# Hybrid decoder step: FFN 1's gate and up products as seven block products for eight, ahead of all of down

## The chip, the cores and the metric

The kernel runs on one core of a Trainium2 chip, as one program. The metric is the device time of an execution in microseconds (us), the median of three runs. The engines are TensorE (PE in the rows; PEld is its weight load), VectorE (DVE), ScalarE (ACT), GpSimd (POOL) and SyncE (SP); SP and ACT issue the DMA transfers.

## The reference, cut to what matters

1032 tokens (1024 of a prompt, 8 samples) of width 1024 go through FFN 1, a mixing stage (RWKV and S5 branches, merged by gates) and FFN 2, all in f32. The change concerns FFN 1 and the norm ahead of it:

```python
def rmsnorm(x, g):
    y = xf * lax.rsqrt(jnp.mean(xf * xf, axis=-1, keepdims=True) + NORM_EPS)
    return (y * g.astype(jnp.float32)).astype(x.dtype)

def swiglu(x, w_gate, w_up, w_down):
    return (jax.nn.silu(x @ w_gate) * (x @ w_up)) @ w_down

x = x + 0.5 * swiglu(rmsnorm(x, p['g_ffn1']), p['ffn1_gate'], p['ffn1_up'], p['ffn1_down'])
```

`FFN_DIM` is 2816, that is 22 tiles of 128 columns of gate and 22 of up.

## The kernel before

Activations lie transposed: x is 8 tiles (`DT`) of 128 features by 1032 tokens. A matmul in f32 is made as three matmuls of rounded parts: every operand is split into a high part (fp32r) and the low rest, and hi x hi, hi x lo and lo x hi are added up in PSUM. So weights and activations each need a copy (high) and a subtraction (low) before TensorE can use them.

**FFN 1** (`ffn_block`, from line 363) works in four groups of 6, 6, 5 and 5 tiles (`FFN_GROUPS`). In a group each turn makes one gate tile and one up tile: two products (`product`, line 199) of 8 k-tiles x 3 parts x 3 token blocks of 344 columns, 72 matmuls each. GpSimd splits the weights of each (lines 179 and 182, `split_units`). VectorE scales both sums by the norm's factor `rstd` (lines 455, 458), multiplies (463) and makes the low part (466); ScalarE makes the silu (534) and the high part (536). After the turns of a group come eight down products over its tiles, which VectorE adds to x in SBUF (492; 482 in the last group). At the program's start ScalarE and VectorE make the high and low parts of g*x, and the squares and their sums in transposed form (lines 254, 270, 273); TensorE adds the sums over the partitions and spreads `rstd`.

**S5 setup.** VectorE also computes tables for the later S5 branch, some 520 small steps of 16 to 256 columns, each waiting for the one before (`s5_setup_dve`, `Steps.do`; lines 600 to 760). They are dealt out by an estimate of their time: up to `SLOT_NS` = 9000 ns of them at the end of a turn (`spend`). Whenever a table is ready ScalarE stores it to DRAM at the beginning of a later turn (`store`, line 837), where it waits for `su_ready`.

**FFN 2** (`strassen_ffn`) has another form already. Gate and up of a tile are one pair; the activations are two token halves (516 columns) by even and odd feature tiles, and a pair takes seven block products of 4 k-tiles x 3 parts x 2 blocks of 258 columns, 24 matmuls each (line 3487, `PROD`), on sums and differences of the blocks. The operands b11, t1, t2, b21, t3, b22 and t4 are made once. For each pair ScalarE makes seven high parts of weights (3366), GpSimd seven low parts (3170) and four sums of weight blocks (3173), 128x512 each. High and low parts lie in a ring of four places, so the parts of a product can be made only a few products ahead. The pair's results: ScalarE copies three partial sums out of PSUM (3394, 3404, 3409) and makes two silus of half width (3417); VectorE adds (`g1a`, `u2a`, `g2a`), scales and multiplies, nine steps of 516 columns (3304 to 3327). TensorE's seventh product (n = 6) waits for `u2a`, the first of the next pair for `g1a`. ScalarE's order in an even pair is: ... copy, high part, silu 1 (waits for VectorE's `g1m`), high part, silu 2; weight work stands behind the silu in its queue. Finished tiles go to DRAM and come back for down (`a_spilled`).

Of the kernel before, what the change touches and what calls it, by code (L numbers as in the profile page):

```python
# [97 lines left out]
def plan(nc, g):  # L98
# [58 lines left out]
    g.a_tiles = 0  # L157

# [91 lines left out]
def square_act(act, g, n, k, tmp):  # L250

    if k >= 2:
        act.wait_ge(g.ssum_step, DT * n + k - 1)
    act.activation(tmp[:, k % 2, :], g.x[:, k, :], ACT.Square).then_inc(g.sq_ready, 1)


def squares_act(act, g, n, ready=None):

    for k in range(DT):
        if ready:  # L260
            ready(k)
        square_act(act, g, n, k, g.tmp)
# [3571 lines left out]
```

## Time and profile before

| | us |
|---|---|
| median of 3 runs (2458.02 to 2460.93) | 2459.64 |
| span of the profiled execution | 2458.0 |
| TensorE busy in it | 2413.0 (98%) |
| VectorE, ScalarE, GpSimd busy | 1287.0, 579.2, 1053.7 |

The profile is of one execution. Its time lies in stages: FFN 1 up to 765 us, the mixing stage up to 1736, FFN 2 to the end. Engines run beside each other, so a stage is read by the engine that is never idle there, and then by what each idle stretch of it waits for. Matmul durations in the rows overlap; the distance from start to start is the cost.

### The profile page before, as it was taken

What the parts mean: (1) busy time and instruction counts of PE and PEld (TensorE: products, weight loads), DVE (VectorE), ACT (ScalarE), POOL (GpSimd) and SP (SyncE); (2) the same over time, 40 slices, a digit from 0 to 9 for tenths busy, and PEclk for the clock granted to TensorE, in tenths of its full rate; (3) what the DMA queues carried; (4) which work ended last, traced back from release to release, by engine and by line L of the source; (5) the groups of instructions that cost most, each with busy time, mean ns of one, the idle gap of its engine ahead of it and who ended that gap; (6) DMA issues with size and microseconds to landing.
All of it is one profiled execution on the core that took longest, in us unless ns stands there. A gap on an engine that the chain in (4) does not pass through costs nothing. (4 is left out here: it accounts for less than half of the span.)

```text
span 2458.0 us, 50034 instructions
## 1 busy us (share of the span) xinstructions
PE 2413.0 (98%) x21418; PEld 2361.5 (96%) x21418; DVE 1287.0 (52%) x1843; ACT 579.2 (24%) x1084; POOL 1053.7 (43%) x604
## 2 busy tenths in 40 slices
PE   8999999999999999999998999999999999999998
PEld 8999999999999999999997888899999999999998
DVE  6851871671336255642466776666754444453225
ACT  4000010010011000010336676412433333341001
POOL 3434444344444344422340000244686868775550
PEclk9999999999999999999999999999999999999998
DMA  3111211111114432623451100062121212143211
GB/s 141 43 53 50 77 60 52 68 53 59 51 38 176 104 93 86 186 79 100 152 190 58 33 18 19 30 243 106 65 104 63 91 70 84 69 181 106 76 52 69
DMA packets 93733, 211.94 MB, mean 86 GB/s; under 512 B 16464, under 2 KB 42704, under 8 KB 92816
## 3 DMA queue, kind: packets, MB, share of 16 engines
q1 hardware_dynamic: 67184, 157.96, 19.2%
q10 hardware_dynamic: 26400, 51.82, 6.5%
q8 instruction: 115, 1.88, 0.3%
q14 instruction: 34, 0.28, 0.0%
HBM read 154.39 MB, written 54.20 MB: 85 GB/s over the span
## 5 line engine op out<-in xcount | busy, mean ns | idle before, releaser
L179 POOL TENSOR_TENSOR whi<-wraw,small 128x1024 fp32r<-128x1024 f32 (+3 forms) x134 | 227.9, 1701 | 844.9 <-PE ps L213 772.1
L213 PE MATMUL ps<-hhi,whi 128*128 128x344 f32 x1848 | 396.3, 323 | 0.0
L213 PE MATMUL ps<-hlo,whi 128*128 128x344 f32 x1848 | 392.9, 321 | 0.0
L213 PE MATMUL ps<-hhi,wlo 128*128 128x344 f32 x1848 | 391.5, 320 | 0.0
L182 POOL TENSOR_TENSOR wlo<-wraw,whi 128x1024 fp32r<-128x1024 f32 (+3 forms) x134 | 324.9, 2425 | 10.5
L213 PEld LDWEIGHTS ps<-hlo,whi 128*128 128x128 f32 x1848 | 313.4, 189 | 0.0
L213 PEld LDWEIGHTS ps<-hhi,whi 128*128 128x128 f32 x1848 | 311.1, 189 | 1.9 <-issue 0.7
L213 PEld LDWEIGHTS ps<-hhi,wlo 128*128 128x128 f32 x1848 | 309.5, 189 | 0.0
L3487 PE MATMUL ps<-t_hi,whi 128*128 128x258 f32 x704 | 143.7, 285 | 3.0 <-ACT ffn_gate L3394 1.0
L534 ACT ACTIVATE tmp<-tmp 128x1032 f32<-128x1032 f32 x22 | 23.5, 1068 | 504.2 <-DVE tmp L455 487.8
L3487 PE MATMUL ps<-t_lo,whi 128*128 128x258 f32 x704 | 142.2, 283 | 0.0
L3487 PE MATMUL ps<-t_hi,wlo 128*128 128x258 f32 x704 | 141.3, 282 | 0.0
L3170 POOL TENSOR_TENSOR wlo<-weights_sum,whi 128x512 fp32r<-128x512 f32 x66 | 92.1, 1395 | 52.7 <-ACT whi L3366 51.4
L3487 PEld LDWEIGHTS ps<-t_hi,whi 128*128 128x128 f32 x704 | 108.7, 189 | 5.0 <-POOL wlo L3170 1.7
L1784 POOL TENSOR_TENSOR sm_v<-sm_v,rw_e 128x2048 f32<-128x2048 f32 x1 | 3.6, 3622 | 253.5 <-DVEq L1547 253.5
L213 PE MATMUL ps<-ahi,whi 128*128 128x344 f32 x528 | 111.9, 320 | 0.0
L213 PE MATMUL ps<-alo,whi 128*128 128x344 f32 x528 | 111.7, 320 | 0.0
L213 PE MATMUL ps<-ahi,wlo 128*128 128x344 f32 x528 | 111.5, 319 | 0.0
L3487 PEld LDWEIGHTS ps<-t_hi,wlo 128*128 128x128 f32 x704 | 109.0, 189 | 0.0
L3487 PEld LDWEIGHTS ps<-t_lo,whi 128*128 128x128 f32 x704 | 108.9, 189 | 0.0
L492 DVE SCALAR_TENSOR_TENSOR x<-ps,x 128x1032 f32 x24 | 29.6, 1233 | 151.4 <-PE ps L213 151.4
L3487 PE MATMUL ps<-b_lo,whi 128*128 128x258 f32 x528 | 106.3, 283 | 0.0
(513 smaller groups left out, 5056.8 us busy)
## 6 DMA issues: line engine op xcount, KB each, us to landing
wraw<-ffn_up SPq DMA_DIRECT2D x44, 512.0 KB, 3.2
wraw<-ffn_down SPq DMA_DIRECT2D x40, 384.0 KB, 3.0
wraw<-ffn_up SPq DMA_DIRECT2D x11, 1024.0 KB, 4.8
weights_raw_b<-ffn_up SPq DMA_DIRECT2D x11, 1024.0 KB, 4.7
a_spilled<-ffn_gate SPq DMA_DIRECT2D x18, 516.0 KB, 2.7
a_raw<-a_spilled SPq DMA_DIRECT2D x18, 516.0 KB, 4.4
wraw<-w_mix SPq DMA_DIRECT2D x18, 512.0 KB, 3.4
gates<-gate_out ACTq DMA_DIRECT2D x16, 516.0 KB, 2.8
```

The costliest lines, as they stand in the source:

```text
L179: pool.tensor_tensor(g.whi[:, s, 0:n], g.wraw[:, s, 0:n], g.zero.to_broadcast([P, n]), ALU.add).then_inc(g.w_hi, 1)
L182: pool.tensor_tensor(g.wlo[:, s, 0:n], g.wraw[:, s, 0:n], g.whi[:, s, 0:n].bitcast(F32), ALU.subtract).then_inc(g.w_split, 1)
L213: last = pe.matmul(g.ps[:, 3 * bank_set + b, 0:BLK], w[:, s, k * P:(k + 1) * P], x(k, b), start=(k == 0 and first), stop=(k == kt - 1 and ...
L492: v.scalar_tensor_tensor(xt, acc(g, j), 0.5, xt, ALU.mult, ALU.add)\
L534: act.activation(g.tmp[:, 0, :], g.tmp[:, 0, :], ACT.Silu).then_inc(g.silu_done, 1)
L1784: st.do(pool.tensor_tensor(V, V, over(E7[:, :, sample]), ALU.mult))
L3170: pool.tensor_tensor(ring(g.wlo, n), source(n), ring(g.whi, n).bitcast(F32), ALU.subtract).then_inc(g.st_lo, 1)
L3487: last = pe.matmul(g.ps[:, b0 + c, 0:QB], ring(w, r, k), x[:, k, c * QB:(c + 1) * QB], start=start and k == 0 and first, stop=k == DT // 2 ...
```

## The change

FFN 1 gets a function of its own, `first_ffn`, in the form that FFN 2 has. All 22 pairs run ahead of all of down. Pair 0 takes eight plain block products (`FIRST_PROD`) while the operands are made, pairs 1 to 21 seven each. Every finished activation tile goes to DRAM; down reads them back in blocks of 6, 6, 6 and 4 tiles, and reads x again from its input. The norm's sums come from a second copy of x, row-major: ScalarE squares nine row tiles with a running sum (`rows_squares`), VectorE takes the root, nine TensorE products spread it. The S5 setup is dealt out anew: up to `PAIR_NS` = 5000 ns after each of pairs 2 to 20 and `DOWN_NS` = 4000 ns after a down unit. x is stored for later in eight parts during the last down units. FFN 2's semaphores get base values; its steps are the same.

The diff, cut to its core:

```diff
+FIRST_HI = [(n, q) for n in ("b11", "b21", "t1", "b22", "t2", "t3", "t4") for q in range(4)]
+FIRST_LO = FIRST_HI[:-4]
+HI0, LO0 = len(FIRST_HI), len(FIRST_LO)
+FIRST_PARTS = ((3, 0, 0), (0, 1, 0), (1, 0, 1), (2, 1, 1))
+FIRST_PROD = ((0, "b11", 2, True, None), (1, "b11", 0, True, None), (2, "b21", 4, True, None), (3, "b21", 6, True, None),
+              (0, "t1", 2, False, "p1"), (1, "t1", 0, False, "q1"), (2, "b22", 2, False, None), (3, "b22", 0, False, None))
+FIRST_BLOCKS = ((0, 6, (0, 1, 2, 3, 4, 5)), (6, 6, (6, 7, 10, 11, 16, 17)), (12, 6, (0, 1, 2, 3, 4, 5)),
+                (18, 4, (8, 9, 15, 16)))
...
+        def rows_squares(n):
+            if n < 8:
+                act.wait_ge(g.gt_in[n // 4], 16)
+                x, total = g.rows[n // 4][:, n % 4, :], g.small[:, 0, n:n + 1]
+            else:
+                act.wait_ge(g.c_in, 16 * 3)
+                x, total = g.rows_end[0:NB, :], g.small[0:NB, 0, n:n + 1]
+            act.activation(x, x, ACT.Square, accum_out=total).then_inc(g.xt_sq, 1)
...
+        def one(i, b, j, between=None):
+            pair, n = 2 * b + j, 7 * j
+            a11, a12, a21, a22 = (part(j, r, c) for r in range(2) for c in range(2))
+            lo(i, b, n)
+            pool.wait_ge(g.st_in[j], i * 16 + 16 * (b + 1))
+            total("s1", sums(0), a21, a22, ALU.add)
+            g.fst_sum.wait(pool, i, pair, "s1")
+            total("s2", sums(1), sums(0), a11, ALU.subtract)
+            lo(i, b, n + 1)
+            total("s3", a21, a11, a21, ALU.subtract)
+            lo(i, b, n + 2)
+            lo(i, b, n + 3)
+            total("s4", sums(1), a12, sums(1), ALU.subtract)
+            lo(i, b, n + 4)
+            lo(i, b, n + 5)
+            if between:
+                between()
+            lo(i, b, n + 6)
+
+        for n, (s, r, c) in enumerate(FIRST_PARTS):
...
+        for n, (s, r, c) in enumerate(FIRST_PARTS):
+            pool.wait_ge(g.st_hi, n + 1)
+            pool.tensor_tensor(place(g.wlo, s), part(0, r, c), place(g.whi, s).bitcast(F32), ALU.subtract)\
+                .then_inc(g.st_lo, 1 if n < 3 else 4)
+        for q in range(4):
+            pool.wait_ge(g.b_mixed, q + 1)
+            pool.tensor_scalar(g.x[:, 2 * q, late], g.x[:, 2 * q, late], gain(2 * q), None, ALU.mult).then_inc(g.b_scaled, 1)
...
+        setup["vector_start"](v, st)
...
+        for pair in range(2, NP):
+            j = pair % 2
+            G, U = halved(g.gate, j), halved(g.upv, j)
+            last = pair == NP - 1
+            done(v, 0, pair, 3)
+            g.fst_copy.wait(v, 0, pair, "p1")
+            on(v.tensor_tensor(G[0], two("y", j), G[0], ALU.add))
+            g.fst_up.wait(v, 0, pair, "g1a")
+            on(v.tensor_tensor(G[0], G[0], R[0], ALU.mult))
+            if last:
+                tile_low(0)
+            done(v, 0, pair, 4)
+            g.fst_copy.wait(v, 0, pair, "p5")
+            on(v.tensor_tensor(U[1], two("x", j), U[1], ALU.add))
+            g.fst_up.wait(v, 0, pair, "u2a")
+            on(v.tensor_tensor(U[1], U[1], R[1], ALU.mult))
+            if last:
+                tile_low(1)
+            done(v, 0, pair, 5)
+            g.fst_copy.wait(v, 0, pair, "u2")
+            on(v.tensor_tensor(G[1], two("z", j), G[1], ALU.add))
+            g.fst_up.wait(v, 0, pair, "g2a")
+            on(v.tensor_tensor(G[1], G[1], R[1], ALU.mult))
+            if last:
+                tile_low(2)
+            done(v, 0, pair, 6)
+            on(v.tensor_tensor(U[0], two("x", j), R[0], ALU.mult))
+            if last:
+                tile_low(3)
+            g.fst_up.wait(v, 0, pair, "u1")
+            g.fst_copy.wait(v, 0, pair, "silu1")
+            on(v.tensor_tensor(G[0], G[0], U[0], ALU.mult))
+            g.fst_copy.wait(v, 0, pair, "silu2")
+            on(v.tensor_tensor(G[1], G[1], U[1], ALU.mult))
+            if last:
+                tile_low(4)
+                tile_low(5)
+            else:
+                setup["vector"](pair, PAIR_NS)
...
+        for pair in range(2, NP):
+            j = pair % 2
+            G, U = ([halves(t[:, j, x]) for x in xa] for t in (g.gate, g.upv))
+
+            def hi(step):
+                for n in SPLIT_AT.get(7 * j + step, ()):
+                    if n < BODY or pair < NP - 2:
+                        hi_of(n, pair - j)
+
+            def silu(half):
+                g.fst_up.wait(act, 0, pair, ("g1m", "g2m")[half])
+                x = halves(g.gate[:, j, xa[half]])
+                on(act.activation(x, x, ACT.Silu))
+
+            setup["scalar"](act, pair)
+            hi(0)
+            if pair == 2:
+                full_silu(0, 1)
+            done(act, 0, pair, 0)
+            act.wait_ge(g.a_out[j], spilled[j] + 16 * (pair // 2))
+            on(act.activation(G[0], two("x", j), ACT.Copy))
+            hi(1)
+            if pair == 2:
+                full_silu(1, 2)
+            done(act, 0, pair, 1)
+            g.fst_up.wait(act, 0, pair - 2, "a2")
+            on(act.activation(U[1], two("z", j), ACT.Copy))
+            hi(2)
+            done(act, 0, pair, 2)
+            on(act.activation(G[1], two("x", j), ACT.Copy))
+            hi(3)
+            hi(4)
+            if pair == NP - 1:
+                for t in range(3):
+                    tile_high(t)
+            hi(5)
+            silu(0)
+            hi(6)
+            silu(1)
+            if pair == NP - 1:
+                for t in range(3, 6):
+                    tile_high(t)
+        for u in range(LAST):
+            b, k = divmod(u, DT)
+            setup["scalar"](act, NP + u)
+            if k < down_size(b + 1):
...
+        for n, (p, name, b0, start, copied) in enumerate(FIRST_PROD):
+            s = FIRST_PARTS[p][0]
+            pe.wait_ge(g.st_lo, p + 1 if p < 3 else 7)
+            if copied:
+                g.fst_copy.wait(pe, 0, 0, copied)
+            last = multiply(lambda k: place(g.whi, s, k), lambda k: place(g.wlo, s, k), name, b0, start, True)
+            if n != 2:
+                last.then_inc(g.st_done, 1)
+
...
+                if pair == 1 and n == 5:
+                    pe.wait_ge(g.rstd_small, 1)
+                    g.fst_up.wait(pe, 0, 0, "u1a")
+                    pe.wait_ge(g.c_in, 16 * 3)
+                    rate(range(8))
+                if pair == 1 and n == 6:
+                    pe.wait_ge(g.rstd_ready, 1)
...
-SLOT_NS = 9000
+PAIR_NS, DOWN_NS = 5000, 4000
```

Two places where the instructions stand otherwise. The first is VectorE at the end of a turn of FFN 1 (before) and of a pair (after); `s_par` is a table of the S5 setup, `ffn_gate` and `ffn_up` are the pair's tiles. Before:

```order
L455 TENSOR_TENSOR tmp<-ps,rstd 128x1032
L458 TENSOR_TENSOR tmp<-ps,rstd 128x1032
L463 TENSOR_TENSOR tmp<-tmp 128x1032
L466 TENSOR_TENSOR alo<-tmp,ahi 128x1032
L672 TENSOR_SCALAR s_par<-s_par 128x16
L670 SCALAR_TENSOR_TENSOR s_par<-s_par 128x16
```

After:

```order
L688 TENSOR_TENSOR ffn_gate<-ffn_gate,rstd 128x516
L692 TENSOR_TENSOR ffn_up<-ps,rstd 128x516
L697 TENSOR_TENSOR ffn_gate<-ffn_gate,ffn_up 128x516
L699 TENSOR_TENSOR ffn_gate<-ffn_gate,ffn_up 128x516
L1076 TENSOR_SCALAR s_par<-s_par 128x16
L1078 TENSOR_TENSOR s_par<-s_par 128x16
```

Four full-width steps ahead of the setup steps have become nine of half width (the last four are shown). The number of setup steps in the slots behind pairs 2 to 20 is 28, 28, 28, 28, 29, 24, 17, 17, 30, 16, 19, 19, 20, 25, 18, 16, 19, 28 and 17.

The second is ScalarE around a store of a table. Before, in FFN 1, it stands between turns:

```order
L536 ACTIVATE ahi<-tmp 128x1032
L837 DMA s_out<-s_out_part 256x1x512
L534 ACTIVATE tmp<-tmp 128x1032
L536 ACTIVATE ahi<-tmp 128x1032
L837 DMA s_turn<-s_turn_part 256x1x512
```

After, at the beginning of pair 12, it stands ahead of the high part of a weight (`whi<-weights_sum`) and the first copy of the pair:

```order
L858 ACTIVATE ffn_gate<-ffn_gate 128x516 x2
L1251 DMA s_turn<-s_turn_part 256x1x512
L761 ACTIVATE whi<-weights_sum 128x512
L866 ACTIVATE ffn_gate<-ps 128x516
L761 ACTIVATE whi<-wraw 128x512
L872 ACTIVATE ffn_up<-ps 128x516
```

What moved: the wait for the setup (`su_ready`) now stands ahead of weight work in ScalarE's queue, which before was GpSimd's alone.

## Rows read from the trace of the kernel before

**Rows 1.** Busy time by stretch: FFN 1, then FFN 2's pairs.

```profile
8.00:762.00 754.00, 752.69 (x4780) 752.32 (x4781) 394.96 (x682) 83.19 (x79) 313.29 (x152) 1.00 0.18 59
1800.00:2160.00 360.00, 359.89 (x2983) 358.75 (x2982) 163.78 (x162) 124.93 (x215) 273.71 (x195) 1.00 0.21 75
```

**Rows 2.** Timeline of TensorE, FFN 1's start and end (start, us, ...).

```profile
8.85 1.23 PE L569 MATMUL ps<-hhi,whi 128*128 128x344 f32 x3 [8.85 <-ACT hhi L317]
...
11.59 0.76 PE L569 MATMUL ps<-hhi,whi 128*128 128x344 f32 x3
...
755.26 0.63 PE L213 MATMUL ps<-ahi,whi 128*128 128x344 f32 x3
...
765.19 0.64 PE L213 MATMUL ps<-hhi,whi 128*128 128x344 f32 x3
```

**Rows 3.** Timeline of TensorE, FFN 2's first pair and first down matmuls.

```profile
1736.03 0.40 PE L3487 MATMUL ps<-b_hi,whi 128*128 128x258 f32 x2
...
2190.45 0.63 PE L3506 MATMUL ps<-a_hi,whi 128*128 128x344 f32 x3
```

**Rows 4.** Timeline of VectorE in FFN 2, pairs 11 to 13.

```profile
1989.13 1.80 DVE L3327 TENSOR_TENSOR ffn_gate<-ffn_gate,ffn_up 128x516 f32<-128x516 f32 x1
1999.57 0.70 DVE L3304 TENSOR_TENSOR ffn_gate<-ps,ffn_gate 128x516 f32<-128x516 f32 x1 [8.65 <-PE ps L3487]
...
2002.44 0.69 DVE L3313 TENSOR_TENSOR ffn_up<-ps,ffn_up 128x516 f32<-128x516 f32 x1 [0.28 <-PE ps L3487]
...
2009.88 0.68 DVE L3327 TENSOR_TENSOR ffn_gate<-ffn_gate,ffn_up 128x516 f32<-128x516 f32 x1
2019.72 0.69 DVE L3304 TENSOR_TENSOR ffn_gate<-ps,ffn_gate 128x516 f32<-128x516 f32 x1 [9.16 <-PE ps L3487]
```

**Rows 5.** Timeline of VectorE, two S5 setup steps in FFN 1.

```profile
299.56 0.23 DVE L688 TENSOR_TENSOR s_tmp<-s_persistent,s_out_part 128x64 f32<-128x64 f32 x1
299.82 1.96 DVE L690 TENSOR_TENSOR s_tmp<-s_par,s_out_part 128x64 f32<-128x64 f32 x1
```

**Rows 6.** Timeline of VectorE and GpSimd, root steps in FFN 2's pair 0.

```profile
1758.00 1.30 POOL L3173 TENSOR_TENSOR weights_sum<-weights_sum,weights_raw_b 128x512 f32<-128x512 f32 x1
1758.19 1.15 DVE L3252 SCALAR_TENSOR_TENSOR small<-small 86x12 f32<-86x12 f32 x1
1759.26 1.30 POOL L3170 TENSOR_TENSOR wlo<-weights_sum,whi 128x512 fp32r<-128x512 f32 x1
1759.37 1.22 DVE L3253 TENSOR_TENSOR small<-small 86x12 f32<-86x12 f32 x1
```

**Rows 7.** Timeline of GpSimd in the same pairs.

```profile
1990.34 1.74 POOL L3173 TENSOR_TENSOR wraw<-wraw 128x512 f32<-128x512 f32 x1
...
1997.80 1.31 POOL L3170 TENSOR_TENSOR wlo<-weights_sum,whi 128x512 fp32r<-128x512 f32 x1 [0.71 <-ACT whi L3366]
...
2003.39 1.63 POOL L3173 TENSOR_TENSOR weights_sum<-weights_sum,weights_raw_b 128x512 f32<-128x512 f32 x1
...
2015.13 1.29 POOL L3170 TENSOR_TENSOR wlo<-weights_raw_b,whi 128x512 fp32r<-128x512 f32 x1 [0.42 <-ACT whi L3366]
2020.42 1.31 POOL L3170 TENSOR_TENSOR wlo<-weights_sum,whi 128x512 fp32r<-128x512 f32 x1 [4.00 <-ACT whi L3366]
```

**Rows 8.** Timeline of ScalarE: silu 1 of pair 12; first weight copy of pair 14.

```profile
2002.19 0.64 ACT L3417 ACTIVATE ffn_gate<-ffn_gate 128x516 f32<-128x516 f32 x1 [2.08 <-DVE ffn_gate L3306]
...
2029.19 0.63 ACT L3366 ACTIVATE whi<-weights_sum 128x512 fp32r<-128x512 f32 x1
```

**Rows 9.** TensorE's wait near the end, and the granted clock in three stretches.

```profile
2445.74 1.33 PE L3706 MATMUL ps<-seg,ssum 128*86 128x1 f32 x8 [2.50 <-DVE ssum L3668]
...
2442.00:2444.00 2.00, 1.24 (x8) 0.95 (x7) 1.08 (x3) 0.10 (x1) 0.00 (x0) 1.00 0.24 88
2444.00:2446.00 2.00, 0.26 (x2) 0.27 (x3) 1.68 (x4) 0.39 (x1) 0.00 (x0) 0.89 0.62 213
2446.00:2448.00 2.00, 1.07 (x8) 0.98 (x7) 0.76 (x5) 0.00 (x0) 0.00 (x0) 0.50 0.62 228
```

**Rows 10.** DMA issues: a finished tile to DRAM (KB each, us to landing).

```profile
a_spilled<-ffn_gate SPq DMA_DIRECT2D x18, 516.0 KB, 2.7
```

In the rows of stretches the columns are: length, busy us (instructions) of TensorE, its weight load, VectorE, ScalarE and GpSimd, the granted clock, the DMA share and GB/s. In timelines: start, us, engine, line, operation, out<-in, shapes, count, and in brackets the idle time before it and what ended it.

More of the change, by code:

```diff
@@ L247, with square_act @@
 RB = 430
-def square_act(act, g, n, k, tmp):
+def square_act(act, g, n, k, tmp, x):
     if k >= 2:
         act.wait_ge(g.ssum_step, DT * n + k - 1)
[L254 to L262, printed above, removed]
+    act.activation(tmp[:, k % 2, :], x[:, k, :], ACT.Square).then_inc(g.sq_ready, 1)
 def square_sum(v, g, n, k, ssum=None, tmp=None):
@@ L839, in store, with scalar @@
            .then_inc(g.su_out[what], 16)
-    def scalar(act, turn):
-        while sent[0] < len(ready) and ready[sent[0]] < turn:
+    def scalar(act, slot):
+        while sent[0] < len(ready) and ready[sent[0]] < slot:
             store(act, sent[0])
@@ L1008, in _ @@
                 u_unit(k)
+            v.wait_ge(g.x_out, 16 * DT)
+            v.wait_ge(g.sq_ready, DT * (n0 + 1))
+            for j in range(2):
+                v.memset(g.raw[:, j, 7:8], 0.0).then_inc(g.zero_ready, 1)
+            v.wait_ge(g.zero_ready, 2)
             for k in range(UT, NU):
@@ L2825 @@
 KEPT = 4
-A0, B0, X0 = FT, 2 * DT, 16
+A0, X0 = FT, 16 * DT
+BH0, BL0 = HI0 + DT, LO0 + DT
+M0, S0, T0 = 16, 4, 4
+DONE0, IN0, OUT0 = 7 * NP, 8 * NP, 16 + 8 * NP
+BACK0 = [16 + 16 * len(range(r, FT, 6)) for r in range(6)]
 SPILLED = NP - KEPT
@@ L2896, in plan_strassen @@
     g.st_in = [S("pair_in0"), S("pair_in1")]
[L2897 removed]
+    sums, copies, steps = S("weight_sums"), S("up_copies"), S("up_steps")
+    g.fst_sum = Laps(sums, SUMS)
+    g.fst_copy = Laps(copies, COPIES, first=[(0, n) for n in ("p1", "q1", "g2", "u2")] +
+                      [(1, n) for n in ("p1", "p5", "u2")] + [(0, "silu"), (2, "p1"), (1, "silu")])
+    g.fst_up = Laps(steps, STEPS, first=[("none", n) for n in range(6)] + [(0, n) for n in ("g1a", "u1a")] +
+                    [(1, n) for n in ("g1a", "u2a", "g2a", "u1")] + [(p, n) for p in range(2) for n in ("gm", "um", "a2")])
+    g.st_sum = Laps(sums, SUMS, base=NP * len(SUMS))
     g.st_hi, g.st_lo, g.st_done = S("part_hi"), S("part_lo"), S("part_done")
[L2899 removed]
+    g.st_copy = Laps(copies, COPIES, base=NP * len(COPIES),
                      first=[(p, n) for p in range(2) for n in ("p1", "p5", "u2")] +
                      [(p, n) for p in range(2) for n in ("silu1", "silu2")])
[L2902 removed]
+    g.st_up = Laps(steps, STEPS, base=NP * len(STEPS),
                    first=[(0, n) for n in ("g1a", "u2a", "g2a", "u1", "g1m", "g2m", "u2m", "a1", "a2")])
@@ L3626, in build @@
     with nc.Block() as block:
-        ffn_block(nc, g, a["ffn1_up"], a["ffn1_down"], V_G1,
-                  before={"sync": first_loads, "scalar": first_x},
-                  setup=s5_setup(g, s5_dram), gnext=V_GMIX, ahead=ahead(a["w_mix"], DT, RT), block=block)
+        first_ffn(nc, g, a["ffn1_up"], a["ffn1_down"], V_G1, V_GMIX, a["x"], a["x_rows"], a["tabs"],
+                  (a["s5_b"], a["s5_c"], a["vec"]), a_dram, x_dram, s5_setup(g, s5_dram), ahead(a["w_mix"], DT, RT),
+                  block)
         proj_block(nc, g, a["w_mix"], a["shift"], f_dram, x_dram, o["last"], s5_dram["in"], a["s5_d"], u_dram, us_dram,
```

849 lines of the change are left out of this document (536 added, 313 removed).

## The prediction

> **What bounds the kernel now.** I read the busy time by stretch first, then the timeline of each engine. In FFN 1 TensorE is busy 752.69 of 754 us, and in FFN 2's gate and up products 359.89 of 360, both at the full granted clock [rows 1]; so the time is the sum of the matmuls, plus every moment in which TensorE waits. FFN 1 runs from its first matmul at 8.85 us to the next block's first at 765.19 [rows 2], 756.3 us. The 21 groups of three matmuls from 755.26 to 765.19 take 0.473 us each, 0.1576 us a matmul [rows 2], so FFN 1's 4752 matmuls (44 products of 72, 22 tiles x 8 x 9 in down) fill 749.0 us. The other 7.3 us are its start. The reader is to see that no other engine counts there now: GpSimd works 313 of the 754 us, VectorE 395 [rows 1].
>
> FFN 2 already has the seven-product form, with nearly the same GpSimd and ScalarE programs, so its rows are the nearest ones for the new FFN 1. Its pair period is 2019.72 - 1999.57 = 20.15 us [rows 4], 2.88 us a product of 24 matmuls. What FFN 2 doesn't have is the S5 setup on VectorE. That is the point of this prediction.
>
> **The change, part by part.**
>
> *Products.* Before, a pair is 144 matmuls of 344 columns: 144 x 0.1576 = 22.7 us. After, 21 pairs of seven block products take 20.15 us each and the first, with eight, 23.0: 446.2 for 499.4 us. Down keeps its 1584 matmuls. **-53.2 us.** By the Trainium skill (TensorE: Matmul & The Clock Gate, Back-to-back issue gap) a matmul stands columns / 2.4 GHz plus 2.5 ns behind the last, 110 and 146 ns here. The rows show 120 and 158, so the measurement decides; by the page 21 pairs would gain 2.5 us each, and the sum would move by 1 us.
>
> *The start.* Half of x's columns are needed first, so the first matmul can come some 1.2 us sooner (before, it waited for a 516 KB tile). But the operands b11 to t4 are now made on ScalarE, VectorE and GpSimd while pairs 0 and 1 run. ScalarE's queue also holds nine row squares, the first of them behind 1 MB of weights and 2 MB of rows. In pair 1 the GpSimd lows of t4 stand ahead of the last product's weights, and TensorE waits there for the reciprocal root too. Pair 2's first copy waits until pair 0's tile has gone to DRAM, 2.7 us in flight [rows 10], after three full-width VectorE steps. FFN 2 did the like in 454.4 us (1736.03 to 2190.45) [rows 3] where 22 x 20.15 = 443.3: 11 us lost. A walk through the queues gives up to 27 us. I take 19, nearer the walk, since FFN 2's operands were begun beside another block's matmuls and these are not. Bounds 8 and 27. Against the 7.3 us of before and the 1.2 us gained: **+10.5 us** (0 to 19).
>
> *S5 setup on VectorE, against GpSimd.* It is 525 small steps. Before, a setup step that begins while a GpSimd instruction runs lasts until that one ends: 0.23 us becomes 1.96 [rows 5]. Of 510 such steps 26 began so and 25 were held; none of the other 484 took over 0.5 us. That cost nothing, GpSimd being free 60% of the time. In FFN 2 GpSimd works 273.71 of 360 us [rows 1], eleven instructions a pair, most of 1.29 us, each starting as the last ends, and small steps of VectorE then get through one for one: 1.15 and 1.22 us where 0.17 would do [rows 6].
>
> Now time from the start of an even pair (1988.1 in FFN 2's trace). VectorE is done with the odd pair before at 2.9 (1989.13 + 1.80) [rows 4] and would begin its setup steps there. GpSimd is busy from there to 9.0 with five instructions, free for 0.7, and busy again until its second sum at about 16.2 (1990.34, 1997.80, 2003.39) [rows 7]; then it waits for a copy on ScalarE that stands behind the silu, and the silu waits for VectorE (2002.19) [rows 8]. So VectorE gets five steps through by 9.1, four in the gap, then one per instruction: 15 by 16.2, and 0.2 to 0.45 us a step after that. But it has 16 to 28 steps there, and TensorE's last product of the pair, due at 17.3, waits for u2a, which needs three VectorE steps of 0.7 after the setup. With 28 steps: 16.2 + 13 x 0.2 + 2.1 = 21.0, a stall of 3.7 us; with 17 wide ones 3.0. Of the nine slots behind odd pairs (3 to 19), two (11 and 17) hold the "ready" of a table late, and ScalarE's store of it stands ahead of the weight copy that TensorE needs 5 us later (2029.19) [rows 8]: 5.3 and 4.9 us. The nine: 3.7 + 3.7 + 3.6 + 3.0 + 5.3 + 3.5 + 3.5 + 4.9 + 4.6 = 36 us. Behind even pairs GpSimd is mostly free (2015.13 + 1.29 to 2020.42 idle) [rows 7] and 29 steps fit in the 9.1 us before VectorE's next work (2010.56 to 2019.72) [rows 4]; only slots 8, 14 and 16 cost, 2.9, 2.3 and 1.8 us, by the store ahead of the copy. **+43 us.** The lower bound is 10 (if the stall hits only where a store waits and the rest fits), the upper 60.
>
> The Trainium skill (SBUF — State Buffer, SBUF: two separate sides) says the pair of ports goes whole to whichever starts first and the other blocks. By it GpSimd too would slip by each small step. In the rows it does not: 1758.00 to 1759.26 with a step let through between [rows 6] is the undisturbed spacing. By the page it would be about 12 x 0.2 = 2.4 us later in each odd slot, where its lead over TensorE is about 0.5 us; that is a rival below.
>
> *The clock.* Stalls of 3 to 5 us are new. At the end of this kernel the granted clock falls to 0.50 of full, 1.2 GHz, in a wait of 2.50 us (1.00, 0.89, 0.50) [rows 9], while waits of 1 us did not do it. At the start the slow clock lasts from 8.85 to 11.59: nine matmuls in 2.74 us for 1.42 [rows 2], so a fall costs 1.3 us. Of some 13 stalls I take six to fall: **+8 us**, from 0 to 17.
>
> *Handover to down.* The low parts of the first six tiles are made inside the last pair by VectorE, with GpSimd splitting down's first weights: **+1.5 us** (0 to 4). Down itself has setup steps for six units of 8.5 us, of which GpSimd fills about 3.3; VectorE may lag there by 3 us and has 8.5. Nothing. The spilled tiles, 22 x 516 KB each way, lie beside 0.18 to 0.21 DMA share [rows 1]: nothing. The last down units are 5.7 us for 7.1 and still above VectorE's 3.5 to 4: nothing, TensorE's own count being the same. The storing of x moves from the next block into the last units and hides likewise.
>
> **The sum.** -53.2 + 10.5 + 43 + 8 + 1.5 = +9.8 us. The profiled execution has a span of 2458.0 us and the median is 2459.64, 1.6 more; both should move alike: **2469.4 us**.
>
> **The rivals.**
> (B) *The setup hides.* If the small steps mostly slip between GpSimd's instructions, only about 10 us of stall remain and the clock stays: 2459.6 - 53.2 + 10.5 + 10 + 1.5 = 2428 us. For it: VectorE itself is busy only 163.78 of 360 us in FFN 2 [rows 1], and 95 us of steps more would fit easily by busy time. Against it: rows 5 and 6.
> (C) *Half of it.* The stall at the last product is 1 to 3 us for each slot (a VectorE step more gets through per gap, or GpSimd runs ahead), in sum 25 us with 3 for the clock: 2446 us.
> (D) *GpSimd slips too*, by the page's rule or by wide steps of 0.43 us: then the low part of the third product comes late as well, 1 to 2 us more in each odd slot, and more stalls drop the clock: +9 to +18 us, about 2483 us. This mechanism decides as soon as GpSimd's lead of 0.5 us in the third product is gone.
> That the change doesn't do what it says is out: the products are there one by one in the program.
>
> **How the numbers follow.** My forecast (2469, give or take 9) has 0.5, B 0.15, C 0.2, D 0.15. The likeliest one's own range is 2458 to 2480. Holding 8 in 10 means taking in C and half of B and of D: 2434 to 2486. About 0.2% (5 us) is what a measurement of this kernel can tell from no change: faster than 2454.7 are B, most of C and a tail of the forecast, 0.34; within are 0.18; slower 0.48.
>
> **What would show it.** In the profile after, (1) FFN 2's rows stay, and FFN 1's undisturbed pairs take 20.15 us; (2) TensorE waits for a VectorE step at product 7 of even pairs, 9 or so times, 3 to 5 us each, alternating with pairs that don't wait; (3) setup steps last 1.2 us one after another; (4) the granted clock shows levels under 1.00 between 80 and 480 us; (5) the first three pairs take about 80 us. The prediction is wrong if TensorE is idle less than 15 us between pair 2 and down, which gives B, or if the first pairs lose as little as FFN 1's start does now.

## The result and the profile after

The changed kernel takes **2504.43 us**, median of 4 runs (2503.43 to 2505.05), against 2460.28 (2458.02 to 2462.46) for the kernel before in the same comparison: ratio 1.018, 95% interval 1.0166 to 1.0195. The direction of the forecast was right, its size was not: 2469.4 was said, with 2486 as the upper end of its range.

The span of the profiled execution is 2503.3 us, 45.3 more than before. By stretch (time, busy time of PE, PEld, DVE, ACT and POOL, granted clock, DMA share, GB/s): pairs 0 to 2, pairs 3 to 20, last pair and down, the rest.

```profile
8.00:94.00 86.00, 74.72 (x543) 73.20 (x544) 64.95 (x73) 45.85 (x78) 55.08 (x38) 0.92 0.42 156
94.00:530.00 436.00, 388.03 (x3023) 384.34 (x3022) 334.17 (x572) 122.57 (x216) 273.37 (x199) 0.93 0.20 73
530.00:808.00 278.00, 272.00 (x1762) 270.05 (x1761) 151.13 (x189) 43.74 (x47) 126.63 (x73) 1.00 0.37 128
808.00:2503.00 1695.00, 1655.94 (x16619) 1604.54 (x16618) 891.07 (x1162) 493.63 (x1002) 736.60 (x446) 0.99 0.30 95
```

Where FFN 1 had TensorE busy without a pause [rows 1], it now lacks 48 of 436 us in the pairs, and the clock there is 0.93 on average. The waits of TensorE between 94 and 531 us (engine, line, what it waited for, total, times, longest):

```profile
PE ps L921 <- POOL wlo L494: 25.7, 7, 6.7
PE ps L921 <- DVE ffn_up L679: 21.8, 6, 4.5
```

Both kinds come from the setup: the second wait is for VectorE's own chain; the first stands behind a store that ScalarE issues only when VectorE's table is ready (the run with late stores below separates them). This is VectorE behind an odd pair (start, duration, line, operation):

```profile
117.56 1.78 DVE L699 TENSOR_TENSOR ffn_gate<-ffn_gate,ffn_up 128x516 f32<-128x516 f32 x1
119.27 1.27 DVE L1040 TENSOR_SCALAR s_par<-s_par 128x16 f32<-128x16 f32 x1
120.57 1.21 DVE L1042 SCALAR_TENSOR_TENSOR s_par<-s_par 128x16 f32<-128x16 f32 x1
...
124.31 0.17 DVE L1049 SCALAR_TENSOR_TENSOR s_par<-s_par 128x16 f32<-128x16 f32 x1
...
130.29 1.15 DVE L1051 TENSOR_SCALAR s_par<-s_par 128x16 f32<-128x16 f32 x1
131.48 0.17 DVE L1049 SCALAR_TENSOR_TENSOR s_par<-s_par 128x16 f32<-128x16 f32 x1
...
134.40 0.69 DVE L672 TENSOR_TENSOR ffn_gate<-ps,ffn_gate 128x516 f32<-128x516 f32 x1
135.13 0.69 DVE L674 TENSOR_TENSOR ffn_gate<-ffn_gate,rstd 128x516 f32<-128x516 f32 x1
135.74 0.69 DVE L679 TENSOR_TENSOR ffn_up<-ps,ffn_up 128x516 f32<-128x516 f32 x1
```

and TensorE at the same place; an undisturbed group of two matmuls starts every 0.24 us, here every 0.43:

```profile
131.94 0.40 PE L921 MATMUL ps<-b_hi,wlo 128*128 128x258 f32 x2
136.56 0.79 PE L921 MATMUL ps<-t_hi,whi 128*128 128x258 f32 x2 [4.22 <-DVE ffn_up L679]
137.15 0.63 PE L921 MATMUL ps<-t_lo,whi 128*128 128x258 f32 x2
...
141.45 0.63 PE L921 MATMUL ps<-t_hi,wlo 128*128 128x258 f32 x2
141.88 0.46 PE L921 MATMUL ps<-b_hi,whi 128*128 128x258 f32 x2
```

The granted clock in product 7 (columns as in the stretches above):

```profile
136.60:141.80 5.20, 5.20 (x24) 5.20 (x25) 2.31 (x3) 1.57 (x3) 4.29 (x3) 0.50 0.00 0
```

Nine steps are long; the short ones lie in GpSimd's gap or behind its last instruction. This is the walk that the prediction made, at the predicted place. What the walk priced too low stands behind the wait: the whole of product 7 runs at half the clock. The pair takes 27.38 us, the one before it 20.16 (starts of VectorE's line 692: 94.58, 114.74, 142.12).

### The profile page after: what moved, and what is told of

It is laid out like the page before. It is cut to its first block and busy times, and to the rows that moved or that the text cites. A ratio compares the mean times of both kernels' runs of the same rounds, so it can differ in the third digit from the quotient of the medians.

```text
span 2503.3 us, 51841 instructions
## 1 busy us (share of the span) xinstructions
PE 2390.7 (96%) x21940; PEld 2332.1 (93%) x21940; DVE 1441.7 (58%) x1993; ACT 708.5 (28%) x1347; POOL 1193.3 (48%) x761
## 5 line engine op out<-in xcount | busy, mean ns | idle before, releaser
L921 PE MATMUL ps<-t_hi,whi 128*128 128x258 f32 x688 | 151.5, 304 | 54.5 <-POOL wlo L494 25.7
L206 PE MATMUL ps<-hhi,whi 128*128 128x344 f32 x816 | 177.4, 326 | 0.0
L206 PE MATMUL ps<-hlo,whi 128*128 128x344 f32 x816 | 174.0, 322 | 0.0
L206 PE MATMUL ps<-hhi,wlo 128*128 128x344 f32 x816 | 173.7, 322 | 0.0
L921 PE MATMUL ps<-t_lo,whi 128*128 128x258 f32 x688 | 148.1, 299 | 0.0
L175 POOL TENSOR_TENSOR wlo<-wraw,whi 128x1024 fp32r<-128x1024 f32 (+1 forms) x60 | 145.0, 2416 | 4.7
L921 PE MATMUL ps<-t_hi,wlo 128*128 128x258 f32 x688 | 147.2, 297 | 0.0
L3916 PE MATMUL ps<-t_hi,whi 128*128 128x258 f32 x704 | 143.8, 285 | 3.0 <-ACT ffn_gate L3823 1.0
L3916 PE MATMUL ps<-t_lo,whi 128*128 128x258 f32 x704 | 142.2, 283 | 0.0
L3916 PE MATMUL ps<-t_hi,wlo 128*128 128x258 f32 x704 | 141.4, 282 | 0.0
L206 PEld LDWEIGHTS ps<-hhi,whi 128*128 128x128 f32 x816 | 137.8, 190 | 1.9 <-issue 0.7
L206 PEld LDWEIGHTS ps<-hlo,whi 128*128 128x128 f32 x816 | 138.8, 190 | 0.0
L206 PEld LDWEIGHTS ps<-hhi,wlo 128*128 128x128 f32 x816 | 137.5, 190 | 0.0
```

Of the source, the lines that this page charges most:

```text
L175: pool.tensor_tensor(g.wlo[:, s, 0:n], g.wraw[:, s, 0:n], g.whi[:, s, 0:n].bitcast(F32), ALU.subtract).then_inc(g.w_split, 1)
L206: last = pe.matmul(g.ps[:, 3 * bank_set + b, 0:BLK], w[:, s, k * P:(k + 1) * P], x(k, b), start=(k == 0 and first), stop=(k == kt - 1 and ...
L921: last = pe.matmul(g.ps[:, b0 + c, 0:QB], w(k), x[:, k, c * QB:(c + 1) * QB], start=start and k == 0 and fresh, stop=k == DT // 2 - 1 and ...
L3916: last = pe.matmul(g.ps[:, b0 + c, 0:QB], ring(w, r, k), x[:, k, c * QB:(c + 1) * QB], start=start and k == 0 and first, stop=k == DT // 2 ...
```

## The experiments

All runs are compared with the kernel before in the same call (median of before 2460.26 to 2460.58). Pairs are read from the start of VectorE's line 692 in one to the next; "pair 2's mark" is the first of these, which closes the start. (Where an edit moves lines, it is the same step under another number.) Times of single stretches come from the one profiled execution of a run; medians are of 4 executions, 10 for the even slots, 2 for the run that prices waits.

**Setup behind even pairs only, behind odd pairs only, in no pair, and the stores late.** The first edit is shown; the second has `== 1`, the third drops the call and has `DOWN_NS = 5300`.

```diff
-                setup["vector"](pair, PAIR_NS)
+                if pair % 2 == 0:
+                    setup["vector"](pair, PAIR_NS)
```

> The S5 setup steps stand only behind even pairs (10 slots of 5000 ns of the estimate, as many steps in each as after has); what stood behind odd pairs goes into down. In after the nine odd slots stall TensorE 4.1 to 4.6 us at product 7 of the next pair, while in even slots GpSimd is held up now and then and the steps take 0.17 us each. Theory 'GpSimd turns' (a small VectorE step starts only when one GpSimd instruction ends, so a slot of 28 steps outlasts the pair only when GpSimd runs without a pause): no product-7 stall is left, even pairs take 20.2 us, and only two or three waits behind a store of setup parts remain; first block about 740 us, kernel 2445 (2438 to 2455). Theory 'too many steps in any slot': even slots would then stall like odd ones once the run of GpSimd shifts, about half of the loss stays: 2470 to 2480. Theory 'the stalls are nothing to do with setup': 2504.

> The mirror of the even-slot kernel: S5 setup steps only behind odd pairs (9 slots of 5000 ns), the rest in down. Theory 'GpSimd turns': all nine product-7 stalls of 4.1 to 4.5 us stay, each followed by about 3 us at the 0.50 clock; only the waits behind stores in even slots go: 2492 (2486 to 2500). Theory 'too many steps in any slot': about half the loss goes, 2470 to 2480.

> No S5 setup step stands in the pairs; all of them stand in down, in slots of 5300 ns of the estimate for 4000. The pairs have then nothing that stalls them: pairs 2 to 20 take 20.15 us each at clock 1.00, which is 73.7 us less than after between 94.6 and 531 us. Down has the whole setup, about twice the steps; GpSimd is 45% busy there and a VectorE slot may take 8 us or more: between 0 and 40 us are lost there. Expected 2435 (2430 to 2470); pairs 2 to 20 alone: 19 x 20.15 = 383 us. Rival 'the stalls come from GpSimd, ScalarE and the weight DMAs of the seven products themselves': stalls at product 7 stay, above 2490.

Measured: even 2455.27 (2453.43 to 2458.84, ratio 0.9978, 0.9969 to 0.9988), odd 2511.94 (1.0211, 1.0194 to 1.0228), none 2477.12 (1.0063, 1.0046 to 1.008). With even slots no wait at product 7 is left and the pairs take 20.16 and 20.52 us in turn, but for two: there TensorE waits 3.13 and 4.17 us for GpSimd's low part behind a store, which costs 12.1 us with the slow clock. With odd slots eight of nine waits at product 7 are there, 4.09 to 4.91 us, and the ninth wait (5.68 us) is one for the low part behind a store. The nth slot holds the same number of steps in both kernels (28, 28, 28, 28, 29, 23, 17, 17, 30). So where a slot stands decides, not how full VectorE is. Behind an even pair (even-slot kernel, the first and the last of 28 setup steps, three of which are still held) GpSimd has pauses of 2.77 and 4.01 us:

```profile
177.75 0.16 DVE L1077 TENSOR_SCALAR s_par<-s_par 128x16 f32<-128x16 f32 x1
...
186.39 0.18 DVE L1130 TENSOR_TENSOR s_persistent<-s_par 128x16 f32<-128x16 f32 x1
```

```profile
179.44 1.29 POOL L494 TENSOR_TENSOR wlo<-weights_raw_b,whi 128x512 fp32r<-128x512 f32 x1 [2.77 <-ACT whi L762]
180.69 1.28 POOL L497 TENSOR_TENSOR weights_sum<-weights_raw_b,weights_sum 128x512 f32<-128x512 f32 x1
...
187.61 1.30 POOL L494 TENSOR_TENSOR wlo<-weights_sum,whi 128x512 fp32r<-128x512 f32 x1 [4.01 <-ACT whi L762]
```

All three took longer than I had expected (2445, 2492, 2435), mainly because down is no free place for setup. It lasts 251.6 us with slots of 2200 or 2600 ns (later runs), 255.3 in after (4000 ns for six units), 263.7 (even) and 267.2 (odd) with 4000 ns up to the end, 295.8 with 5300 (none), where 249.6 is its count of matmuls. The rest of the kernel behind FFN 1 took longer too, 1698.9, 1698.2 and 1701.9 us against 1695.4 in after; no run shows why. In the run with 5300 ns the steps of a unit keep VectorE from adding the unit before:

```profile
637.54 1.23 DVE L718 SCALAR_TENSOR_TENSOR x_down<-ps,x_down 128x1032 f32<-128x1032 f32 x1
```

```profile
638.87 1.20 PE L995 MATMUL ps<-a_hi,whi 128*128 128x344 f32 x3 [5.66 <-issue]
```

The pairs of that kernel are free of setup: 20.16 and 20.51 us in turn, all at clock 1.00. The 0.35 us of the second kind stand at the beginning of the third product of every even pair, where a group of matmuls starts 0.49 us behind the last instead of 0.24, and the next 0.34. TensorE waits for GpSimd's low part, which took 1.75 us beside VectorE's wide steps, and 1.29 elsewhere:

```profile
117.60 1.75 POOL L494 TENSOR_TENSOR wlo<-weights_sum,whi 128x512 fp32r<-128x512 f32 x1
118.92 0.40 PE L921 MATMUL ps<-t_hi,wlo 128*128 128x258 f32 x2
119.41 0.51 PE L921 MATMUL ps<-t_hi,whi 128*128 128x258 f32 x2
```

In the fourth the call that issues the stores goes to the end of ScalarE's pair:

```diff
-            setup["scalar"](act, pair)
             hi(0)
...
             silu(1)
+            setup["scalar"](act, pair)
```

> As after, but ScalarE issues the stores of setup parts at the end of its pair and not at its start, where it waits for VectorE's setup steps with six weight splits queued behind. Theory: the waits of TensorE for the weight low parts (seven, 25.7 us together, after a store) go in even slots (about 11 us with their clock), while in odd slots the product-7 stall of 4 us and its 3 us of clock come in their place: 2487 (2482 to 2494). Rival 'the store waits are the whole of those seven stalls': minus 44 us, 2460. Rival 'the store's place is all one': 2504.

Measured: 2496.29 (ratio 1.0147, 1.013 to 1.0164), 8.1 us less than after, where 17 were expected. The even slots' waits are gone; in odd slots the waits at product 7 take the place of the four store waits and come to the same (107.6 us for these four pairs, 107.2 in after). So 8 us of the loss are the store's place; the rest of the waits in the pairs is the steps'.

**The start.** First VectorE's two Newton refinements ahead of its wait for product 5; then also three of ScalarE's row squares moved up.

```diff
         first_root()
+        newton()
+        newton()
+        v.sem_inc(g.rstd_small, 1)
         done(v, 0, 1, 4)
```

> As after, but VectorE does the second and third Newton step of the norm's root (six steps on 128x9) right behind the first one, ahead of its wait for product 5 of the second pair. In after it stands idle 3.77 us there, and then takes the six while GpSimd is busy, five of them at 0.99 to 1.23 us; TensorE waits 4.06 us for the last. Theory 'GpSimd turns, in the start too': the wait goes, with the slow clock behind it; pair 2 begins about 7 us sooner and the kernel takes 2497 (2494 to 2500). Rival 'the chain of rstd, gate product, spill and copy is what holds the second pair': the 4.06 us come back in front of product 3 of pair 2, 2502 to 2505.

> The Newton steps early and, beside it, three of ScalarE's squares of rows of x (tiles 4 to 6) in its three idle stretches of 1.6 to 2.8 us before 39.6 us, ahead of the copies that TensorE waits for at 43.27 us (2.69 us) and of the high parts it waits for at 52.65 us (1.98 us). Theory: ScalarE's queue is what both waits hang on; with their slow clock they are worth 4 to 7 us beside the first edit: 2491 (2487 to 2495). Rival 'VectorE's chain of sums is behind both waits': within 1 us of the kernel with the Newton steps alone.

Measured: 2502.40 (ratio 1.0168, 1.0152 to 1.0185) and 2504.29 (1.0177, 1.016 to 1.0194), against 2504.43 for after: nearer the rivals, though the second lies 1.9 us from the first and not within 1. Neither differs from after by more than the noise (the ratios' intervals overlap). The wait of 4.06 us for the root went, and the one for ScalarE's copy in pair 2 grew from 1.64 to 3.51 and 4.43 us; the wait at 43.3 us did not shorten (2.69, then 2.56). Over the seven profiles with the early roots pair 2's mark is at 89.2 to 93.6 us, over the six without at 93.4 to 94.6. I had said -7 us for the kernel; the median moved by -2.

**All that the theory says, together.** Even slots 5000 ns, odd slots 1250 ns (4 to 8 small steps in the run), down 2600 ns, stores late, the start's two edits.

```diff
+                setup["vector"](pair, PAIR_NS if pair % 2 == 0 else ODD_NS)
+PAIR_NS, ODD_NS, DOWN_NS = 5000, 1250, 2600
```

> All that the theory says together: 5000 ns of setup behind even pairs, only 1250 ns (7 small steps) behind odd pairs, the rest in slots of 2600 ns in down, the stores at the end of ScalarE's pair, the Newton steps and squares early. The odd slot has about 9 us up to the next copy; at one step per GpSimd instruction of 1.26 us seven steps fit. Theory: no stall of over 0.5 us between pair 3 and pair 20, pairs 20.2 and 20.5 us in turn, down loses 6 us and not the 14 of the even-slot kernel: 2424 (2419 to 2434), below before. If VectorE's steps of any number there stall TensorE: about 2450. If the gain of the even slots came from something else than the number of steps: above 2455.

Measured: **2430.60** (2427.31 to 2433.69), ratio 0.9881, 0.9865 to 0.9898: faster than both kernels. Its pairs and down:

```profile
89.00:477.00 388.00, 385.70 (x3195) 383.63 (x3193) 301.27 (x461) 132.78 (x229) 295.25 (x207) 1.00 0.25 90
477.00:729.00 252.00, 250.06 (x1586) 249.29 (x1587) 184.33 (x299) 35.43 (x34) 114.65 (x65) 1.00 0.38 127
```

All setup steps are there (518, as in after), and TensorE waits for nothing of over 0.5 us between pair 3 and pair 20. I had said 2424, up to 2434; the profiled execution took 2427.31, the others 2429.73 to 2433.69. Several edits went in at once here, and the run alone doesn't divide the gain among them; the runs above and below do for slots and stores.

**What a wait costs.** No setup in the pairs; ahead of the step `u2a`, in pairs 4, 6, ... 20, VectorE makes 3 to 12 copies that compute nothing.

```diff
+            for _ in range(LADDER.get(pair, 0)):
+                st.do(v.tensor_copy(g.stm[:, :].rearrange("p r a c -> p (r a c)"), g.rstd[:, 0:512]))
             done(v, 0, pair, 4)
```

> No setup in the pairs (slots of 5300 ns in down, stores late). In its place VectorE makes 3, 4, 5, 6, 7, 8, 9, 10 and 12 idle copies of 128x512 (not part of the computation) ahead of the step that product 7 waits for, in pairs 4, 6, ... 20. It measures what a wait of each length costs TensorE with the clock behind it, in pairs that are otherwise 20.51 us. If a copy takes its own 0.7 us the waits run from 0 to about 5 us, if each waits for a GpSimd turn from 0.5 to 11 us. Theory 'a fall costs more the longer the wait': beside the wait itself nothing up to about 1.5 us, 1.6 to 1.8 us at 2.4 to 3, 2.6 to 3.0 us from 4 us on. Rival 'each fall costs the same' (my prediction's 1.3 us): 1.3 us at every length.

Measured (2533.83 us, median of 2): each wait in the profiled execution, the pair's time, and what of its excess over 20.51 us is not the wait:

| copies | wait at product 7, us | pair, us | beside the wait, us |
|---|---|---|---|
| 3 | 0.89 | 21.65 | 0.25 |
| 4 | 2.32 | 23.09 | 0.26 |
| 5 | 3.73 | 26.74 | 2.50 |
| 6 | 4.19 | 27.36 | 2.66 |
| 7 | 4.65 | 27.72 | 2.56 |
| 8 | 5.11 | 27.93 | 2.31 |
| 9 | 5.56 | 28.01 | 1.94 |
| 10 | 6.03 | 28.13 | 1.59 |
| 12 | 6.92 | 29.85 | 2.42 |

```profile
175.46 0.51 PE L923 MATMUL ps<-t_hi,whi 128*128 128x258 f32 x2 [2.32 <-DVE ffn_up L681]
```

```profile
220.12 0.79 PE L923 MATMUL ps<-t_hi,whi 128*128 128x258 f32 x2 [3.73 <-DVE ffn_up L681]
```

The granted clock around these two waits:

```profile
170.00:178.00 8.00, 5.68 (x48) 5.48 (x47) 7.41 (x8) 0.98 (x2) 5.65 (x5) 1.00 0.31 122
218.00:224.00 6.00, 3.88 (x18) 3.89 (x19) 3.95 (x5) 1.16 (x2) 1.66 (x2) 0.53 0.00 0
```

Neither theory holds at every length. The cost does not grow with the wait and is not 1.3 us: either the clock doesn't fall and the wait costs 0.25 us beside itself, or it falls and the cost is 1.6 to 2.7 us. Each length stands here once, so the table doesn't say where the border lies, and the other runs show that the length alone does not set it. In after a wait of 2.35 us cost 1.65 us and one of 1.82 us 0.45; in the last run, with the stores back, one of 1.95 us cost 1.42 and the clock fell (first TensorE's row, then the stretch):

```profile
409.27 0.51 PE L921 MATMUL ps<-t_hi,whi 128*128 128x258 f32 x2 [1.95 <-POOL wlo L494]
```

```profile
409.00:413.00 4.00, 3.73 (x19) 3.73 (x20) 0.00 (x0) 0.89 (x2) 3.92 (x4) 0.61 0.24 87
```

In the pairs of all profiles no wait up to 1.91 us was followed by a fall; from 1.95 us on every one was, except the 2.32 us above, and cost 1.2 to 3.0 us beside itself. Waits of 4.1 to 4.3 us at product 7 alone cost 1.7 to 2.7. Rows 9 had shown a fall in a wait of 2.50.

**Is it GpSimd's turns?** Odd slots of 2500 ns (10 to 15 small steps in the run), and the same with every GpSimd instruction of the pairs cut in two. The edit of the low parts is shown; the sums have the same loop.

```diff
+            for h in (slice(0, 2), slice(2, 4)):
+                ins = pool.tensor_tensor(ring(g.wlo, n)[:, h], source(n)[:, h], ring(g.whi, n)[:, h].bitcast(F32), ALU.subtract)
+            ins.then_inc(g.st_lo, 1)
```

> The short-odd-slot kernel with 2500 ns (13 or 14 small steps) behind odd pairs for 1250 ns (7), down at 2200. By the rows of after the thirteenth small step of such a slot ends 11.0 us behind its start and the fourteenth 12.2 us; VectorE's chain up to product 7 has room for about 11. Theory 'turns' : waits of 0 to 1.5 us in the early odd slots, hardly any slow clock, 2440 (2433 to 2447). If the room were 14 us or more: 2430.

> The 2500 ns odd slots again, but every instruction of GpSimd in the pairs (low parts and sums, 128x512) is made as two of 128x256, same work. Theory 'one VectorE step per GpSimd instruction': the setup steps come every 0.65 to 0.8 us for 1.2, the odd slots fit again and the time goes back to that of the short slots, 2431 (2427 to 2436), unless the doubled fixed costs make GpSimd late. Rival 'a share of the memory's bandwidth' or 'steps slow while GpSimd is busy at all': steps stay at 1.2 us, time as with whole instructions.

Measured: whole 2441.78 (ratio 0.9924, 0.9908 to 0.9941), with waits at product 7 of 1.30, 1.30, 1.45, 1.32 and 1.76 us (three more are about 0.4) and the pairs at 20.16 and 20.5 to 22.5; halved 2437.35 (0.9914, 0.9898 to 0.9931). First the whole, then the halved kernel, at the beginning of the same slot:

```profile
116.91 1.27 DVE L1040 TENSOR_SCALAR s_par<-s_par 128x16 f32<-128x16 f32 x1
118.21 1.22 DVE L1042 SCALAR_TENSOR_TENSOR s_par<-s_par 128x16 f32<-128x16 f32 x1
119.46 1.21 DVE L1044 SCALAR_TENSOR_TENSOR s_par<-s_par 128x16 f32<-128x16 f32 x1
```

```profile
112.62 0.70 DVE L1044 TENSOR_SCALAR s_par<-s_par 128x16 f32<-128x16 f32 x1
113.35 0.66 DVE L1046 SCALAR_TENSOR_TENSOR s_par<-s_par 128x16 f32<-128x16 f32 x1
114.04 0.66 DVE L1048 SCALAR_TENSOR_TENSOR s_par<-s_par 128x16 f32<-128x16 f32 x1
```

```profile
114.63 1.45 POOL L495 TENSOR_TENSOR wlo<-weights_sum,whi 128x256 fp32r<-128x256 f32 x2
116.03 1.44 POOL L495 TENSOR_TENSOR wlo<-wraw,whi 128x256 fp32r<-128x256 f32 x2
```

The small step's length follows the length of GpSimd's instruction, 1.21 to 0.66 us, at unchanged work of its own; a share of bandwidth would not do that. All waits at product 7 are gone. The median fell by 4.4 us and not by 11, which is not clear of the noise (the intervals overlap); the traces show the mechanism, not the time. The same weights now take GpSimd 1.40 us instead of 1.25, and TensorE waits for its low parts once in every second pair, 0.95 to 1.03 us (these pairs last 21.4 us).

**Two leftovers.** The last eight columns of `rstd` made inside product 7 of pair 1, and the stores back at the start of ScalarE's pair, both on the 2430.6 us kernel.

> The short-odd-slot kernel with one edit in the start: the last eight columns of rstd (two matmuls of 8x128) are made after half of product 7 of the second pair and not after it, and VectorE copies them ahead of its wait for that product. They begin the chain of gate and up product, silu, spill and copy on which product 3 of pair 2 waited 2.98 us. Theory 'the chain sets the end of the start': it begins 1.4 us sooner or more, pair 2 begins 1 to 3 us sooner, kernel 2428 (2426 to 2430). Rival 'the start is held by the weights of GpSimd': no change, 2430.6.

> The short-odd-slot kernel with ScalarE's stores of setup parts back at the start of its pair, as in after. Theory 'a store holds six weight splits behind it': two or three waits of 2 to 4 us for weight low parts come back, each with 1.4 to 2 us of slow clock: 2443 (2436 to 2450). Rival 'with short slots the store finds its parts done': 2430.6.

Measured: 2431.32 (0.9883, 0.9867 to 0.99), no change; and 2442.85 (0.9928, 0.9911 to 0.9944), 12 us more, 10.3 of them in the four pairs with waits of 1.25 to 2.42 us for `wlo`: the store holds the six weight splits behind it with short slots too. Why the start doesn't give shows in the first. Its edit did not bring the chain of full-width steps forward (66.13 us, 66.16 in the kernel it was built on). All kernels with the early root steps begin that chain several us sooner than after, here 6.7, but beside GpSimd (first VectorE, then GpSimd):

```profile
66.13 1.64 DVE L652 TENSOR_TENSOR ffn_gate<-ffn_gate,rstd 128x1032 f32<-128x1032 f32 x1
67.69 2.32 DVE L653 TENSOR_TENSOR ffn_up<-ffn_up,rstd 128x1032 f32<-128x1032 f32 x1
70.05 2.22 DVE L656 TENSOR_TENSOR ffn_gate<-ffn_gate,ffn_up 128x1032 f32<-128x1032 f32 x1
```

```profile
66.63 2.29 POOL L497 TENSOR_TENSOR wraw<-wraw 128x512 f32<-128x512 f32 x1
68.88 2.30 POOL L494 TENSOR_TENSOR wlo<-weights_sum,whi 128x512 fp32r<-128x512 f32 x1
```

In after GpSimd was idle there and the same three took 1.23 us each:

```profile
72.80 1.23 DVE L652 TENSOR_TENSOR ffn_gate<-ffn_gate,rstd 128x1032 f32<-128x1032 f32 x1
```

So 2.5 of the 6.7 us go back at once, and pair 2 asks for its copy sooner as well: the wait there is 4.42 us instead of 1.64.

## Why the prediction was wrong, and where it was right

The 45.3 us of the profiled execution against the +9.8 of the sum:

| term | forecast | measured | how |
|---|---|---|---|
| products | -53.2 | -53.2 | the forecast's count of matmuls at full clock; undisturbed odd pairs take 20.16 us |
| start | +10.5 | +15.0 | pairs 0 to 2 lose 22.6 us instead of 19; first matmul at 8.58 us, before at 8.85 |
| setup stalls | +43 | +47.1 | twelve waits in pairs 3 to 20 |
| clock in the pairs | +8 | +23.4 | 73.7 lost - 47.1 waits - 9 x 0.35 for the even pairs |
| even pairs | 0 | +3.2 | 20.51 instead of 20.16 us, also without setup |
| handover and down | +1.5 | +7.2 | 1.46, 1.20 and 0.62 us at the handover; the rest in down |
| rest of the kernel | 0 | +2.6 | 1695.4 instead of 1692.8 us |

**The step that failed is the clock.** "A fall costs 1.3 us. Of some 13 stalls I take six to fall." The twelve waits cost 1.95 us each beside themselves, 23.4 us in all, more than the 17 of my upper bound and 15.4 of the 35.5 us by which the sum was short. That this is the clock shows in the trace itself: between 94.6 and 531.0 us the granted clock is at its low level for 58.0 us, 10.9 of them inside the waits; half of the other 47.1 is 23.6. Both halves of the term were mis-sized. Eleven of the twelve waits were followed by the low level, all but the one of 1.82 us; six of thirteen was a hedge with no row behind it, since rows 9 had a fall at 2.50 us and the walk itself put eleven of the twelve stalls at 2.3 us or above. And the 1.3 us came from the first matmuls of rows 2, where TensorE ran at the low level from the outset and rose after 2.74 us; behind a wait of 4.2 us it runs at the low level from 136.56 to some 141.9, and half of these 5.3 us is lost. The Trainium skill (TensorE: Matmul & The Clock Gate, Terms) gives the loss as the time that TensorE spends at the low clock times one minus the granted share, here one half. By it these 5.3 us are 2.7, an estimate; this pair lost 27.38 - 20.51 - 4.22 = 2.65 us beside its wait. Twelve falls at 1.3 us would have made 15.6 us.

The clock alone does not carry the time out of the range. With 23.4 in the place of 8 the sum would have said 2484.8 us, just under the upper end of 2486. The other 20.1 us lie in five terms that all missed to the same side.

**The even pairs** were put at nothing because the pair period of 20.15 us was read from one pair of FFN 2 [rows 4]. The next pair in the same trace, against 2019.72, takes 20.41:

```profile
2040.13 0.69 DVE L3304 TENSOR_TENSOR ffn_gate<-ps,ffn_gate 128x516 f32<-128x516 f32 x1 [8.63 <-PE ps L3487]
```

FFN 2's pairs take 20.15 and 20.33 to 20.52 us in turn. The new FFN 1 loses 0.35 us in each even pair, at the third product, where the prediction had given GpSimd a lead of 0.5 us.

**The setup stalls** were sized well in sum: 39.9 us in the nine odd slots where 36 were forecast, and 7.2 in slots 8, 14 and 16 where 7.0 were (3.04, 2.35 and 1.82 us; forecast 2.9, 2.3 and 1.8). Slot by slot part of it is luck: slots 3 to 9 took 4.1 to 4.4 us instead of 3.0 to 3.7, slots 11 and 17, with a store, 6.7 and 6.5 instead of 5.3 and 4.9, and slots 13 and 19 2.9 and 2.4 instead of 3.5 and 4.6. That GpSimd's turns make the waits at product 7 is shown by four runs (even, odd, 2500 ns, halves). The seven waits for the low part, 25.7 of the 47.1 us, need the store's place as well: with the stores late the three in even slots go and the four in odd slots become waits at product 7.

**The start** was too low by 4.5 us: 1.2 us were claimed for an earlier first matmul, which became 0.27, since it waited for the first low part of VectorE (`b_lo`), and the loss of 22.6 us lay between my 19 and the walk's 27. **Handover and down**: "Nothing" was wrong for the setup in down. In after it cost up to 4 us, in the first three runs, with more of it there, 12 to 44. The **rest of the kernel** took 1695.4 to 1701.9 us in the thirteen profiles with the new FFN 1 and 1692.8 in that of before.

By the list of what would show it: (1) holds for odd pairs, while even ones take 20.51; (2) holds in five of nine odd slots, with waits of 4.12 to 4.55 us for VectorE's step; in the other four TensorE waits for GpSimd's low part; (3) holds, 1.21 us; (4) holds, 0.93 between 100 and 500; (5) pairs 0 to 2 took 86 us and not 80. Rival D's mechanism (GpSimd slips too) is there for wide steps, also without any setup, and not for the small ones it was priced with; its time, 2483, was nearest, but for the wrong reason. For B the odd slots would have had to be short, as in the 2430.6 us kernel.

What stays open: the 2.6 us and more behind FFN 1, why the clock fell in one wait of about 2 us and not in another, and why the seven profiles with the early root steps differ by up to 4 us at pair 2's mark.

## What to carry to other kernels

Count what small steps of VectorE cost in GpSimd instructions, not in their own time: while GpSimd ran without a pause, one step passed per instruction, so they belong where GpSimd waits. A stall that a walk finds has a second half on TensorE's clock: here every wait but one from 1.95 us on cost 1.2 to 3.0 us more, and none up to 1.91 us over 0.5, so price both, and rather trim a slot until the wait is well under 2 us than spread the same work evenly. Read a period that alternates from two neighbours, not from one. A store that waits for another engine's result belongs behind the weight work in its queue.

## What the runs showed of the hardware that I had not expected

- The hold is mutual for wide steps. A 128x1032 product on two SBUF operands took 2.32 us instead of 1.23, and the GpSimd instruction beside it 2.29 instead of 1.28; a 128x512 copy took 1.37 to 1.52 us beside GpSimd (42 of the 64 idle copies) and 0.43 alone (22). Small steps of 0.17 us left GpSimd's instructions 1.25 us apart (median of 52 in after), as without them (median of 36 in the no-setup kernel). The Trainium skill (SBUF — State Buffer, SBUF: two separate sides) says that the pair of ports goes whole to whoever starts first and the other blocks. The wide steps agree with it. The small ones show only one half: they wait for GpSimd, and GpSimd does not come later by the 0.17 us of each; no run shows why.
- A VectorE step that reads PSUM and one SBUF operand is not held. In the no-setup kernel 47 of them lie wholly inside a GpSimd instruction and took 0.68 to 0.70 us each, as alone, and the GpSimd instruction shown here took its usual 1.28; the step with two SBUF operands above took 1.78. One of them:

```profile
128.03 1.28 POOL L497 TENSOR_TENSOR weights_sum<-weights_raw_b 128x512 f32<-128x512 f32 x1
128.36 0.69 DVE L679 TENSOR_TENSOR ffn_up<-ps,ffn_up 128x516 f32<-128x516 f32 x1 [1.43 <-PE ps L921]
```

- TensorE's clock can fall or not at nearly the same wait: 2.32 us cost 0.26 us beside itself, 2.35 us 1.65 and 1.95 us 1.42.
